# Two modulation vectors move from the first layer's panels into its attention, and small moves around the last attention and the gates

## The reference

```python
mod = silu(c) @ ada_w[i] + ada_b[i]            # 1024 -> 6 * 1024
sh_a, sc_a, g_a, sh_f, sc_f, g_f = split(mod, 6)
h = rms_norm(x, attn_norm[i]) * (1.0 + sc_a) + sh_a
y = mixer(h)                                    # layer 0: sparse_mixer, 1024 -> 2840 -> 1024
x = x + g_a * y
h = rms_norm(x, ffn_norm[i]) * (1.0 + sc_f) + sh_f
x = x + g_f * swiglu(h, ...)
```

## Time and profile before

| | |
|---|---|
| median of 3 runs | 1558.48 us (1557.81 to 1564.18) |
| the profiled execution's own time | 1558.25 us |
| its span in the profile | 1556.4 us |
| TensorE, VectorE, ScalarE busy | 1476.5, 1060.7, 757.4 us |
| mean granted clock of TensorE | 0.982 |
| moved by DMA | 331 MB, 213 GB/s over the span |

### The profile page before, as it was taken

One profiled execution on the slowest core, in us unless ns is written; L12 is line 12 of the kernel. 1 busy time (PEld: TensorE's weight loads), 2 busy tenths in 40 slices (PEclk: granted clock), 3 DMA queues, 4 the chain that ended last, 5 costly groups with the idle time before them and its releaser, 6 DMA issues.

```text
span 1556.4 us, 21198 instructions
## 1 busy us (share of the span) xinstructions
PE 1476.5 (95%) x8559; PEld 1193.9 (77%) x8559; DVE 1060.7 (68%) x1637; ACT 757.4 (49%) x1207; POOL 0.2 (0%) x4
## 2 busy tenths in 40 slices
PE   5989999999999889999999999999999998999997
PEld 3757868888877666788777888778888886778886
DVE  3566747886569766566577665688877896476655
ACT  3434635444555545334355554465546624465543
POOL 0000000000000000000000000000000000000000
PEclk9999999999999899999999999999999999999999
DMA  9993064886655747885765855658776523146552
GB/s 361 345 339 137 29 215 164 278 284 218 233 204 187 263 172 249 291 304 187 271 224 186 289 182 199 205 189 287 267 276 241 189 81 109 57 146 192 181 198 80
DMA packets 167842, 331.05 MB, mean 213 GB/s; under 512 B 8120, under 2 KB 109120, under 8 KB 167744
## 3 DMA queue, kind: packets, MB, share of 16 engines
q1 hardware_dynamic: 140928, 230.90, 43.8%
q10 hardware_dynamic: 26816, 98.79, 17.5%
HBM read 328.61 MB, written 1.05 MB: 212 GB/s over the span
## 4 chain that ended last, share of the span: by engine, by line
PE 79%; DVE 12%; DMA 4%; ACT 2%; issue 2%; SPq 0%; ACTq 0%; DVEq 0%
PE ps L2084 21%; PE ps L1978 12%; PE ps L1980 12%; PE ps L1979 12%; PE ps L2085 11%; DMA ring<-in_ada_w_dram 3%; PE ps L1915 2%; DVE wlo L1212 2%; DVE work L1310 1%; DVE res L1312 1%; PE ps L2190 1%; PE ps L2164 1%; PE ps L2267 1%; DMA work<-in_ada_w_dram 1%; PE ps L2279 1%
## 5 line engine op out<-in xcount | busy, mean ns | idle before, releaser
L1212 DVE TENSOR_TENSOR wlo<-wraw,whi 128x1024 fp32r<-128x1024 f32 (+1 forms) x412 | 483.8, 1216 | 151.5 <-ACT whi L680 150.7
L680 ACT ACTIVATE whi<-wraw 128x1024 fp32r<-128x1024 f32 (+1 forms) x412 | 411.0, 1045 | 335.6 <-PE ps L2085 194.8
L2084 PE MATMUL ps<-hT,whi 128*128 128x512 f32 x1472 | 519.8, 398 | 1.9 <-DVE hT L1383 1.9
L2085 PE MATMUL ps<-hT,wlo 128*128 128x256 f32 x1472 | 412.0, 280 | 0.0
L2084 PEld LDWEIGHTS ps<-hT,whi 128*128 128x128 f32 x1472 | 277.1, 188 | 74.7 <-issue 7.0
L2085 PEld LDWEIGHTS ps<-hT,wlo 128*128 128x128 f32 x1472 | 278.5, 189 | 0.0
L1978 PE MATMUL ps<-whi,act_hi 128*128 128x512 f32 x560 | 219.1, 391 | 0.0
L1979 PE MATMUL ps<-wlo,act_hi 128*128 128x512 f32 x560 | 218.0, 389 | 0.0
L1980 PE MATMUL ps<-whi,act_lo 128*128 128x512 f32 x560 | 218.0, 389 | 0.0
L1978 PE MATMUL ps<-whi,hT 128*128 128x512 f32 (+2 forms) x416 | 161.5, 388 | 6.1 <-DVE hT L1383 5.7
L1979 PE MATMUL ps<-wlo,hT 128*128 128x512 f32 (+2 forms) x416 | 158.5, 381 | 0.0
(11 more groups left out here) (233 smaller groups left out, 1309.9 us busy)
## 6 DMA issues: line engine op xcount, KB each, us to landing
wraw<-in_mlp_w_dram SPq DMA_DIRECT2D x96, 1024.0 KB, 5.4
ring<-in_ada_w_dram ACTq DMA_DIRECT2D x82, 1024.0 KB, 6.5
wraw<-in_ffn_w_gate_dram SPq DMA_DIRECT2D x22, 1024.0 KB, 5.4
wraw<-in_ffn_w_up_dram SPq DMA_DIRECT2D x22, 1024.0 KB, 6.8
wraw<-in_ffn_w_down_dram SPq DMA_DIRECT2D x22, 1024.0 KB, 4.9
wraw<-in_diff_w_in_dram SPq DMA_DIRECT2D x12, 1024.0 KB, 5.1
work<-in_ada_w_dram ACTq DMA_DIRECT2D x10, 1024.0 KB, 10.8
wraw<-in_sp_w_in_dram SPq DMA_DIRECT2D x8, 1024.0 KB, 11.7
```

What stands on the lines that cost most here:

```text
L680: nc.scalar.activation(whi[:, u % 2, part], raw_view(u)[:, part], ACT.Copy).then_inc(hi_ready, 1)
L1212: nc.vector.tensor_tensor(wlo[:, u % 2, part], raw_view(u)[:, part], whi[:, u % 2, part].bitcast(F32), ALU.subtract).then_inc(lo_ready, 1)
L2084: mm(ps[:, bank, :], whi[:, u % 2, c0:c0 + P], hT[:, :, k, :], start=(k == 0), stop=False, skip_group_check=True)
L2085: ins = mm(ps[:, bank, 0:S], wlo[:, u % 2, c0:c0 + P], hT_hi[:, k, :], start=False, stop=(k == KT - 1), skip_group_check=True)
```

## The change

- **Vectors 3 and 4 leave the panels.** The panels now hold the four units of vector 2 only, ahead of units 1 and 3 of `in0_0` and `in0_1`. Vector 3 stands in the place of the 14 idle products. Vector 4's first two units stand beside step 12 of `attention(0)`, the others behind its last step. Vector 5's units stand 0, 1, 1, 2 ahead of the units of `out0` (before 1, 1, 1, 1).
- **Where they land.** Units 14, 15, 18 and 19 land in `hT`'s 2 MB, which nobody reads between the panels and `out_turn(0)`; ScalarE issues 14 and 15 after TensorE has finished the panels, 16 to 19 behind the compressed branch's `Silu`, 20 and 21 beside step 13. Units 8 and 9 are issued beside `in0_2`'s last unit, not before the panels.
- **New waits.** VectorE does `vector_out(3)` between `cmp_blocks` and the rest of the heads; TensorE waits for it (`mod_rows` 4) ahead of line 2351. The second half of the compressed rows is added before the head's take of step 12, not after it. `vector_out(4)` follows `out_turn(0)`.
- **Last attention.** The second unit of `out3` is split in halves, on ScalarE beside steps 1 and 3, on VectorE beside steps 3 and 5. One `Exp` of a single element is put on ScalarE behind `ring_fill(94)`.
- **All ten gates.** The four products of a gate are issued column half by column half, not bank by bank. The second of a bank still waits for its first.

```diff
         res = sb("res", [P, 2, TT, D])
+        HT_AT = nc.sbuf_base
...
         ps = stack.enter_context(nc.psum_tensor("ps", [P, 8, 512], F32))
+        hT_raw = nc.alloc_sbuf_tensor_at("hT_raw", [P, 2, 2048], F32, offset=HT_AT)
...
         IDLE_ROWS = 4
-        IDLE_LINK = 14
...
-        STEP_PLAN = [(g, j) for g in range(6) for j in range(4)] + [(9, 2), (9, 3)] + [(10, j) for j in range(4)] + [(11, 0), (11, 1)]
+        STEP_PLAN = [(g, j) for g in (0, 1, 2, 5) for j in range(4)] + [(9, 2), (9, 3)] + [(10, j) for j in range(4)] + [(11, 0), (11, 1)]
...
         FIRST_UNITS = 8
-        IN0_STEPS = {"in0_2": (0, 0, 0, 1), "in0_0": (1, 1, 1, 1), "in0_1": (1, 2, 2, 2)}
+        IN0_STEPS = {"in0_2": (0, 0, 0, 0), "in0_0": (0, 1, 0, 1), "in0_1": (0, 1, 0, 1), "out0": (0, 1, 1, 2)}
+        HT_SLOTS = {14: 0, 15: 1, 18: 0, 19: 1}
...
         x_full = [sem("x_full0"), sem("x_full1")]
+        hT_full = [sem("hT_full0"), sem("hT_full1")]
...
         for r in range(RING_UNITS):
-            slot = ("early", r) if r in EARLY else ("x", WORK_SLOTS[r]) if r in WORK_SLOTS else ("ring", r % 2)
+            slot = ("early", r) if r in EARLY else ("x", WORK_SLOTS[r]) if r in WORK_SLOTS else ("hT", HT_SLOTS[r]) if r in HT_SLOTS else ("ring", r % 2)
...
                 return wk((r - EARLY.start) * 2048, 2048)
+            if kind == "hT":
+                return hT_raw[:, n, :]
...
             kind, n = ring_slot[r]
-            return {"early": early_full, "x": x_full, "ring": ring_full}[kind][n], 16 * slot_use[r]
+            return {"early": early_full, "x": x_full, "hT": hT_full, "ring": ring_full}[kind][n], 16 * slot_use[r]
...
             norm_columns((1,))
-            ring_fill(FIRST_UNITS + 1)
...
             nc.scalar.activation(trig[:, :, :, :], trig_t[:, :, :, :], ACT.Sin).then_inc(sem("trig_ready"), 1)
-            ring_fill(FIRST_UNITS + 2)
...
             norm_columns((3,))
-            row_segment("in0_2", ada=True)
+            row_segment("in0_2", ada=True, beside=lambda i: ring_fill(FIRST_UNITS + 2) if i == 3 else None)
...
             next_panel()
+            act.wait_ge(unit_done, panel_end[2])
+            ring_fill(16)
...
             ins.then_inc(sem("cmp_silu"), 1)
+            ring_fill(20)
...
                     nc.scalar.activation(cmp_s, cmp_s, ACT.Exp, scale=float(HD) ** -0.5).then_inc(sem("cmp_exp"), 1)
+                if i == 13:
+                    ring_fill(22)
...
             ring_fill(94)
+            nc.scalar.activation(mark[0:1, 2:3], mark[0:1, 3:4], ACT.Exp)
...
             def beside_steps(i):
-                if i == 1:
-                    split_unit(o_unit + 1)
+                if i in (1, 3):
+                    split_half(o_unit + 1, i // 2)
...
             nc.vector.memset(hidr[:, :], 0.0).then_inc(sem("hidr_zero"), 1)
+            vector_out(3)
...
                     nc.vector.tensor_tensor(vbd, ps[:, LINK_BANK, :], const("headmask"), ALU.mult).then_inc(sem("cmp_vbd"), 1)
+                if i == 12:
+                    dve.wait_ge(sem("cmp_pv"), 2)
+                    compressed_rows(1)
...
                     nc.vector.tensor_tensor(flat, flat, cmp_m[:, :].rearrange("p (h c) -> p h c", c=1).to_broadcast([P, 16, 16]), ALU.mult).then_inc(sem("cmp_p"), 1)
-                if i in (10, 12):
-                    t = (i - 10) // 2
-                    dve.wait_ge(sem("cmp_pv"), t + 1)
-                    compressed_rows(t)
+                if i == 10:
+                    dve.wait_ge(sem("cmp_pv"), 1)
+                    compressed_rows(0)
...
             out_turn(0)
+            vector_out(4)
...
             def beside_steps(i):
-                if i == 1:
-                    split_unit(o_unit + 1)
+                if i in (3, 5):
+                    split_half(o_unit + 1, i // 2 - 1)
...
                 pe.wait_ge(mod_rows, 6 * l + 3 * f + 3)
-                for h in range(2):
-                    for c_ in range(2):
+                for c_ in range(2):
+                    for h in range(2):
...
                         beside(i)
+                if stage == 0:
+                    vector_units(4, 2, 4)
...
             gate()
-            idle_products(D_BANKS[2], IDLE_LINK)
+            vector_units(3, 0, 4)
...
             pe.wait_ge(sem("cmp_blocks"), 1)
+            pe.wait_ge(mod_rows, 4)
...
                     ins.then_inc(sem("cmp_turned"), 1)
+                if i == 12:
+                    pe.wait_ge(sem("cmp_taken"), 2)
+                    vector_units(4, 0, 2)
...
             attention(0, beside=compression)
-            pe.wait_ge(sem("cmp_taken"), 2)
```

## The result

The changed kernel takes 1540.51 us (median of 4 runs, 1538.59 to 1542.26) against 1559.54 (4 runs, 1557.81 to 1564.18): a ratio of 0.9867, 95% interval 0.9838 to 0.9896. Its profiled execution took 1539.54, with a span of 1537.7.

The account below looks back on a forecast made before the run. TensorE was taken to bound the kernel, with 79% of the chain. The terms −13.0 + 1.0 + 5.0 − 2.8 − 4.3 − 3.0 = −17.1 us, from 1558.25, gave 1541.1 us, range 1533 to 1550.

Parts of the forecast that it names:

- steps 1 and 2: Panels: vector units leave, one wait of 2.7 remains, −13.0 us; half a clock dip behind that wait, +1.0 us.
- the stretch of 54 to 58 us: Sign for the panels: time from 53.3 to the last product of `in0_1`.
- the idle time before the first vector unit: Sign for the panels: TensorE waits for unit 8, put at 2.7 us.
- The measured duration is the one I use: Panels: unit 8 takes the 11.5 us measured for unit 10 from issue to use, not some 7 by the queue rule.
- no wait in the panels: Rival: unit 8 is there at 63.4 and SP's small rows end earlier; −20.8 us in all, 1537.5, chance 0.16.
- From the panels to the attention (3): Panels' end to first attention: VectorE's heads, held behind vector 3, make TensorE wait; +5.0 us, bounds 3 and 9.
- E: End of the third panel on TensorE: 122.7 before, forecast at 109.7.
- End of the attention (4): First attention's end and `out_turn`: vector 4 fills waits, transposes run at full clock; −2.8 us, ends +1 and −3.5.
- Last attention (5): Last attention: halved, spread split saves 4.9 in the first steps, 0.6 given back; −4.3 us, ends −5 and −2.5.
- Gates (6): All gates: new order makes each 0.6 shorter, counting at five in effect; −3.0 us, ends −1 and −4.5.
- three conditions under which the forecast was to be called wrong: Third panel's end later than 114, heads ending over 27 us behind it, or last attention and gates together under 4.
- parts 5 and 6: Last attention's halved split, −4.3 us, and the gates' new order, −3.0 us.

Follow-up runs that it names:

- units_early: Changed kernel with vector units 8 and 9 issued where the kernel before issues them, between the first norm's column blocks: 1539.73 us, ratio 0.9865.
- gates_back: Changed kernel with the old order of a gate's four products alone: 1548.22 us, ratio 0.9928.
- vectors_back: Kernel before with only the new gate order, the half splits of the last attention and the `Exp`, vectors not moved: 1549.42 us, ratio 0.9938.
- vec4_together: Changed kernel with all four units of vector 4 in step 12 of the first attention, its last wait left empty: 1539.99 us, ratio 0.9888.
- split_back: Changed kernel with the whole split of the last attention in its step 1 again: 1540.90 us, ratio 0.9886.
- units_late: Changed kernel with the DMAs of units 8 and 9 issued one step later, in the first step of `in0_0`: 1559.39 us (one run).
- tuned: Changed kernel with half of vector 3 before the fourth transposes, a memset moved, more idle products before layer 1's heads and last gate: 1536.90 us, ratio 0.9872.

## Why the prediction was right, and where it wasn't

**Panels and dip (steps 1 and 2).** −12.0 forecast, −15.8 measured, −16.4 without the first unit's clock. Of the 4.4 between the forecast and the last of these, 3.7 are the wait of 2.7 and its dip of 1.0: neither came. The other 0.7 or so are in the units, which with their vectors took 52.9 where 53.7 had been added up. So two signs of the prediction failed: the stretch of 54 to 58 us, and the idle time before the first vector unit. The failed step is the sentence "The measured duration is the one I use": 11.5 us had been measured in another moment's traffic (510 small packets in the window, 48 here), and unit 8 landed after 8.3. Which part of that traffic made the 11.5 isn't known; small packets alone don't (`units_early`). The rival "no wait in the panels" described this, and also said why SP's rows would be through earlier.

**From the panels to the attention (3).** +5.0 forecast, +4.0 measured, within the bounds and by the steps named: the panel's copies end at E + 3.7 (3.5 forecast), `cmp_blocks` at E + 9.7 (9.8), L2367 starts at E + 12.1 (12.5), `query_heads0` at E + 22.1 (23). With the old gate (`gates_back`) it is 25.3 − 20.2 = 5.1: 0.7 of the missing 1.1 is the first gate, which I had called hidden, and 0.4 is the clock behind the wait. The gate was hidden before the change (20.2 with either order, before and `vectors_back`) and no longer is, since vector 3 now stands behind it.

**End of the attention (4).** −2.8 forecast, −4.0 measured. `out_turn` to the first product gave 3.3, as worked out (3.4). The 0.6 by which the vector units should delay `out_turn` didn't come: from the attention's start to it the traces have 55.3, 55.3 and 56.6 against 56.4, and in the one with 56.6 the granted clock of the first 10 us was 0.70 and not 0.85. The transposes ran at full clock, but filling the last wait, the reason given, isn't needed for it (`vec4_together`).

**Last attention (5).** −4.3 forecast, −3.8 and −3.9 measured (three traces; `split_back`), with the idle time and the steps of 4.4 where they were looked for. The 4.9 of the first steps came as worked out; 1.1 were given back, at a step of 5.5 us with a wait of 0.9 in it, where I had put 0.6. The times show none of it, only the traces.

**Gates (6).** −3.0 forecast. The four gates of the table add up to −2.9, but by chance: 1.4 of the second gate's 2.1 are the clock, 0.77 before and 1.00 after, since with the old order at full clock (`gates_back`) it is 6.0 against 5.3. At equal clock the order gives 0.7 to 0.8 at five gates, the first, second, fourth, seventh and ninth, so about 3.6, near the 3.8 of `gates_back`'s trace. The length of a group (1.5) was right; of which gates count, the first was misjudged, and the gain of the fifth goes into a wait for a DMA. The last doesn't pay: its stretch is 5.5 with either order at full clock and grew by 0.7 in the three traces, with the granted clock at 0.73 in the first.

**The sum.** The stretches of the table come to 22.5; the time won is 18.9 by the traces and 19 to 21 by the medians of runs on one chip. That the total was met (1540.5 for 1541.1) is in good part chance: the stretches of the vectors' move came to −15.8 and not −9.8, and what made up for most of these 6.0 is the rest of the kernel, 3.6 longer, and the 0.5 that the last attention brought less. None of the three conditions under which the forecast was to be called wrong came true: E is 106.2, the heads end at E + 22, and parts 5 and 6 brought 7.4.

## What to carry to other kernels

A landing time read from one row is the price of that moment's traffic; before it is carried to another moment, count what else is in flight there, and give both ends until then. When a wait goes, look again at every edit that was "hidden": the cover can be what was removed. A shorter piece of one engine's work can end in a wait for a load that nobody had looked at, as behind the fifth gate. And compare distances between landmarks in several traces before a difference of a few us is called a loss, or a gain.

## What the hardware showed that I had not expected

- Pairs of products at a granted clock of 1.00 start every 347 or every 353 ns, for tens of us at a time, and one program shows either in the same stretch from one execution to the next. Over the long stretches it makes up to 7 us (931.0 to 937.9). What chooses was not found.
- The first product (by `wlo`) starts between 28.7 and 33.1 us after the span's start in ten of the fourteen traces and between 36.3 and 36.6 in the other four; the changed kernel has both.
- The clock behind a wait can differ with the execution. `vec4_together` is the changed kernel up to the first attention; yet behind the same wait of 2.2 us ahead of the fourth group of transposes its first gate starts at E + 7.6 and not at E + 6.4 as in the changed kernel's three traces: the twenty transposes took 3.95 us and not 2.8. It can also be steady. Behind the wait of 2.95 us (2.72 in `tuned`) the next eight transposes took 1.09 us in all three traces of the changed kernel, in `split_back` and in `units_early`, and 1.97 in both kernels with half of vector 3 ahead. Filled, they took 1.04 both times.
